# Value transposes in pairs between half tiles, and value scaling on ScalarE in a backward sweep

## The reference

```python
def mixer(xs_, ctx):                     # second block
    z, xx, bx, cx, dtx, u = ssm_project(hx, w_in, conv_w, conv_b, dt_bias)
    y_f = ssd_chunked(xx, dt_f, a_f, bx, cx, s_f)       # forward scan
    y_b = ssd_chunked(rev(xx), rev(dt_b), a_b, rev(bx), rev(cx), s_b)
    y = y_f + rev(y_b) + d_skip * xx
    y = rmsnorm(y * silu(z), groups of 512)             # two groups
    pm = pool_mixer(u, pool_w, pool_scale)              # box means minus u, then a matmul
    return concat([y, pm]) @ w_out

def ssd_chunked(xs, dt, a, b, c, h0):    # per chunk of 128 tokens, 16 heads of 64
    y_off = (c @ state) * exp(acs)                      # what earlier chunks give
    state = state * exp(acs[last]) + b.T @ (xs * weight)  # weight: one number per token and head
    y_diag = (c @ b.T * decay) @ (xs * dt)              # inside the chunk
```

## Time and profile before

| what | value |
|---|---|
| median of three runs | 2821.09 us |
| profiled execution | 2826.55 us, its span 2824.8 us |
| TensorE busy | 2659.1 us, 94% of the span |
| VectorE busy | 1638.1 us, 58% |
| GpSimd busy | 995.2 us, 35% |
| ScalarE busy | 609.5 us, 22% |
| backward sweep | about 1544 to 1717 us of the span |
| phase 6, up to the second product loop | about 1849 to 1980 us |

### The profile page before, as it was taken

One profiled execution on the slowest core, in us unless ns is written; L12 is line 12 of the kernel. 1 busy time (PEld: TensorE's weight loads), 2 busy tenths in 40 slices (PEclk: granted clock), 3 DMA queues, 4 the chain that ended last, 5 costly groups with the idle time before them and its releaser, 6 DMA issues. The chain is left out here.

```text
span 2824.8 us, 32083 instructions
## 1 busy us (share of the span) xinstructions
PE 2659.1 (94%) x12350; PEld 2143.5 (76%) x12350; DVE 1638.1 (58%) x2219; ACT 609.5 (22%) x884; POOL 995.2 (35%) x523
## 2 busy tenths in 40 slices
PE   8889999999999999987888999889989999999997
PEld 5778777778888888866776766678767888888885
DVE  6887555756556665676846995653375222222248
ACT  4222242311110011133232104532131110001111
POOL 2122125554333343541212331113645333333353
PEclk9999999999999999998999999989999999999998
DMA  4111142222322332231001332351332111111123
GB/s 138 40 52 44 52 142 82 97 82 97 97 90 89 104 97 94 94 103 64 31 30 38 104 112 75 79 197 45 112 97 83 52 52 45 52 45 52 45 75 105
DMA packets 87332, 224.68 MB, mean 80 GB/s; under 512 B 27392, under 2 KB 30592, under 8 KB 87232
## 3 DMA queue, kind: packets, MB, share of 16 engines
q1 hardware_dynamic: 51232, 168.61, 18.0%
q10 hardware_dynamic: 34848, 50.50, 5.7%
q0 software_dynamic: 1152, 4.19, 0.9%
HBM read 193.79 MB, written 28.31 MB: 79 GB/s over the span
## 5 line engine op out<-in xcount | busy, mean ns | idle before, releaser
L221 POOL CAST w_hi<-w_raw 128x1024 fp32r<-128x1024 f32 x254 | 289.4, 1139 | 1691.1 <-PE ps L234 1672.0
L230 PE MATMUL ps<-a_hi,w_hi 128*128 128x512 f32 x2080 | 698.5, 404 | 51.2 <-PEq L3028 14.6
L223 POOL TENSOR_TENSOR w_lo<-w_raw,w_hi 128x1024 fp32r<-128x1024 f32 x254 | 695.7, 2739 | 20.3
L232 PE MATMUL ps<-a_lo,w_hi 128*128 128x512 f32 x2080 | 680.2, 395 | 0.0
L234 PE MATMUL ps<-a_hi,w_lo 128*128 128x512 f32 x2080 | 679.1, 394 | 0.0
L230 PEld LDWEIGHTS ps<-a_hi,w_hi 128*128 128x128 f32 x2080 | 391.2, 192 | 157.7 <-issue 68.6
L234 PEld LDWEIGHTS ps<-a_hi,w_lo 128*128 128x128 f32 x2080 | 396.7, 191 | 85.2
L232 PEld LDWEIGHTS ps<-a_lo,w_hi 128*128 128x128 f32 x2080 | 397.5, 191 | 83.9
L232 PE MATMUL ps<-g_b,w_hi 128*128 128x512 f32 x1216 | 412.1, 390 | 0.0
L230 PE MATMUL ps<-g_b,w_hi 128*128 128x512 f32 x1088 | 363.8, 392 | 11.5 <-DVE g_b L1812 11.5
L234 PE MATMUL ps<-g_b,w_lo 128*128 128x512 f32 x1088 | 361.5, 389 | 0.0
(11 more groups left out here) (476 smaller groups left out, 2641.2 us busy)
## 6 DMA issues: line engine op xcount, KB each, us to landing
w_raw<-in_wstream SPq DMA_DIRECT2D x254, 512.0 KB, 3.5
ada_w<-in_ada_w ACTq DMA_DIRECT2D x25, 512.0 KB, 3.5
ada_w_b<-in_ada_w ACTq DMA_DIRECT2D x25, 512.0 KB, 3.4
x_res_b<-in_xT SPq DMA_DIRECT2D x2, 2048.0 KB, 11.4
x_block<-x_res_b SPq DMA_DIRECT2D x16, 256.0 KB, 3.1
y_by_token<-y ACTq DMA_DIRECT2D x8, 512.0 KB, 3.3
z_rows<-ada_w ACTq DMA_DIRECT2D x8, 512.0 KB, 2.6
u_rows<-pad ACTq DMA_DIRECT2D x8, 512.0 KB, 4.3
```

What stands on the lines that cost most here:

```text
L221: pool.tensor_copy(k.w_hi[:, s, :], k.w_raw[:, s, :]).then_inc(k.w_high, 1)
L223: pool.tensor_tensor(k.w_lo[:, s, :], k.w_raw[:, s, :], k.w_hi[:, s, :].bitcast(F32), ALU.subtract).then_inc(k.w_split, 1)
L230: pe.matmul(o, w_hi, a_hi[:, c], start=first, stop=False)
L232: pe.matmul(o, w_hi, a_lo[:, c], start=False, stop=False)
```

## The change

Phase 5: VectorE no longer multiplies the values by their own weight, and no longer weighs the next chunk's values in the sweep. ScalarE does both, head by head: 16 ACTIVATEs of 64 columns each, with a per-partition scale (`own_values`, `weigh_next`). A new semaphore `y_own` lets VectorE's sum wait for the first. Phase 6: the 64 value transposes no longer stand in one piece between the halves of pooled tile 0. They stand in four pairs of groups: behind tile 0, between the halves of tile 1, behind tile 1, between the halves of tile 2. The column sums of the squares move from behind tile 1 to behind tile 2, the spread from the middle of tile 2 to the middle of tile 3. ScalarE's squares and copies are put in the matching order.

```diff
+            def own_values(i):
+                if i:
+                    act.wait_ge(s["y_back"], 16 * i)
+                else:
+                    act.wait_ge(s["x_done"], CC)
+                for h in range(SSM_HEADS):
+                    ins = act.activation(heads(y_even[:, :])[:, h, :], values(NC - 1 - i)[:, h, :], ACT.Copy,
+                                         scale=v.own[:, NC - 1 - i, h:h + 1])
+                ins.then_inc(s["y_own"], 1)
+
+            def weigh_next(i):
+                c, r = (NC - 2 - i, 1) if i < NC - 2 else (0, 0)
+                act.wait_ge(s["x_done"], back + BWD_JOBS * i + 2)
+                for h in range(SSM_HEADS):
+                    ins = act.activation(heads(xw[:, :])[:, h, :], values(c)[:, h, :], ACT.Copy,
+                                         scale=v.w_st[:, c, SSM_HEADS * r + h:SSM_HEADS * r + h + 1])
+                ins.then_inc(s["xw_ready"], 1)
...
+            own_values(0)
             act.wait_ge(s["cleared"], 2)
             for i in range(NC):
                 c, t = NC - 1 - i, KT - 1 - i
                 act.wait_ge(s["y_ready"], i + 1)
                 act.dma_start(d.y_tok[c, :, :], y_even[:, :]).then_inc(s["y_back"], 16)
+                if c:
+                    weigh_next(i)
                 n = u_tile(i)
...
                 if t % 2 == 0 and t:
                     load_area(t // 2 - 1)
+                if i + 1 < NC:
+                    own_values(i + 1)
...
-                dve.wait_ge(s["y_back"], 16 * i)
-                ch.link(tt(heads(y_even[:, :]), values(c), bc(v.own[:, c, :], 2, HDIM), ALU.mult))
                 dve.wait_ge(s["x_done"], back + BWD_JOBS * i + 1)
                 tt(heads(back_tmp), heads(Xf[0]), per_head(v.e_acs, c, 1), ALU.mult).then_inc(x_free[0], 1)
                 dve.wait_ge(x_free[0], back // 2 + i + 1)
+                dve.wait_ge(s["y_own"], i + 1)
                 tt(y_even[:, :], y_even[:, :], back_tmp, ALU.add).then_inc(s["y_ready"], 1)
                 if c:
                     dve.wait_ge(s["x_done"], back + BWD_JOBS * i + 2)
                     sum_state(c, 1, 1)
-                    if c > 1:
-                        weigh(c - 1, 1)
-                    else:
-                        weigh(0, 0)
...
-        def value_transposes():
+        def value_transposes(first):
             pe.wait_ge(s["y_in"], 16)
-            for t in range(KT):
+            for t in range(first, first + 2):
...
             if m == 0:
-                value_transposes()
                 pe.wait_ge(s["plo"], KT)
-            if m == 2:
+            if 1 <= m <= 2:
+                value_transposes(4 * m - 2)
+            if m == PG - 1:
                 spread(0)
                 spread(1)
...
-            if m == 1:
+            if m < 2:
+                value_transposes(4 * m)
+            if m == 2:
                 square_sums(0)
                 square_sums(1)
...
+        squares(range(0, 2))
         pooled_part(0)
+        squares(range(2, 4))
         pooled_part(1)
+        squares(range(4, KT))
+        pooled_part(2)
         root(0)
         root(1)
         for t in range(0, 4):
             high(t)
-        pooled_part(2)
+        pooled_part(PG - 1)
```

More of the change, by code:

```diff
@@ L2390, in phase5 @@
         s = signals(nc, ctx, "p5", "chain xw_ready moving_ready d_done chosen e_ready w_ready cb_done cb_ready off_done fore_ready "
-                                   "st_done state_ready diag_done y_ready y_back y_out0 y_out1 u_in0 u_in1 u_in2 u_in3 z_out d_out "
+                                   "st_done state_ready diag_done y_ready y_own y_back y_out0 y_out1 u_in0 u_in1 u_in2 u_in3 z_out d_out "
                                    "dhi dlo x_done x_free0 x_free1 cleared area_in pooled")
@@ L2914, in scalar, with squares @@
         act.wait_ge(s["dlo"], len(LATE))
[L2915 to L2919, removed]
+        def squares(ts):
+            for t in ts:
+                act.wait_ge(x_free[t % 2], t // 2 + 1)
+                if t >= 2:
+                    act.wait_ge(s["added"], t - 1)
+                act.activation(w.tmp[:, t % 2, :], yz[:, t, :], ACT.Square).then_inc(s["sq"], 1)
         def pooled_part(m):
@@ L2942, in scalar @@
             high(t)
-        pooled_part(2)
+        pooled_part(PG - 1)
         for t in range(4, KT):
             high(t)
-        for m in range(3, KT):
+        for m in range(PG, KT):
             pooled_part(m)
```

## The result

The changed kernel takes 2831.64 us (2824.51 to 2836.71, seven runs), the kernel before, beside it, 2821.09 (2818.49 to 2828.03, seven runs). The ratio over all these runs is 1.0028, with an interval of 1.0016 to 1.0040: 7.9 us slower, between 4.5 and 11.3 (the two medians alone lie 10.6 apart). The interval lies above 1; the difference is just under the 0.3% taken as the bound of what can be told from no change. The profiled spans are 2824.8 and 2831.2 us, 6.4 apart.

A forecast was written before the change was run, and what follows sets the result against it. The prediction took TensorE to bound the kernel, with short stretches where another engine feeds it late. The sweep's +16 and phase 6's -10 gave +6 us on the median of 2821.09, so 2827 us, own range 2819 to 2834.

The forecast's parts named there:

- the +16: Phase 5, backward sweep: with both sets of scalings on ScalarE it ends 16 us later.
- the relief: Sweep: with VectorE partly idle, some stretching of its two-SBUF-input operations goes; -3 us, between 0 and -5.
- The pairs: Phase 6: value transposes in four pairs between half pooled tiles, none waiting; 10 us gained.
- The later spread: Phase 6: sums, roots and spread one pooled tile later in TensorE's order cost nothing, with 28 us of cover.
- the 12 that the forecast named for that case: Phase 6: upper end of the gain, 12 us, if the half clock around the sums goes too.
- The set of 3.95 us: Sweep: one set of 16 64-column ACTIVATEs on ScalarE takes 3.95 us.
- the rival of 4.8 us: Sweep: a set costs 4.8 us, the 128-column spacing; +18 net, 2839 us; chance 16%.
- The ring of 11.4 us a step: Sweep: chain pooled tile, own set, sum, weighing set, copy, pooled tile; 11.4 us a step beside the pooled tile.
- these three terms: Sweep: step 0 +1.7, steps 1 to 6 +22.7, step 7 -9.1; sum +15.3 us.
- the late TensorE of +3.5: Sweep: late state for steps 3, 5, 6 slows TensorE, so the last u tile is late; +3.5 us, 0 to +6.
- Nothing of the 16 us is taken back: Forward scan: it cannot start without the sweep's end, so it recovers none of the 16 us.
- The faster rival: Sweep: sets lie beside other work, TensorE alone bounds it; needs sets under about 2.8 us; 2804 us; chance 12%.

The follow-up runs named there:

- the sixth experiment: Kernel before, with all 64 value transposes in one piece moved from between the halves of pooled tile 0 to behind it; 2824.01 us, ratio 1.0006.
- the last experiment: Changed kernel with the own-weight set right behind the copy of the u tile and the weighing back on VectorE; 2813.61 us, ratio 0.9966 to the kernel before.
- the second experiment: Kernel before with only the scaling moved to ScalarE, phase 6 left as it was; 2840.2 us, ratio 1.0056.
- the fourth experiment: Changed kernel with the weighing set moved behind the copy of the u tile; 2829.15 us, ratio 1.0016 to the kernel before.
- The third experiment: Changed kernel with the own-weight set moved right behind the copy of the u tile; 2814.05 us, ratio 0.9958 to the kernel before.

## Why the prediction was right, point by point

**The direction and the size.** Forecast +6 on 2821.09; the spans differ by 6.4, the runs by 7.9. The two terms were +16 and -10, and they measured +17.2 and -10.1. Each came from the place and the cause that the forecast named. That the +16 came so close is in part luck: inside it one term was too small and another was not paid, as the point on the relief below shows.

**The pairs: right.** Not one pair waits. The first starts 16.5 us behind the third group of pool products (1895.57 - 1879.09, the latter TensorE's first row there); by the forecast's 1879.3 and the 1862.79 of before it was to be 16.5. The later spread was hidden, with 26.7 us of cover where 28 were worked out, and pooled tile 3 is copied out 10.1 us sooner from the phase's start. The forecast gave the 4.21 us wait and the region pace one sum and could not split them; the sixth experiment splits them. The lower clock behind the column sums stayed in the kernel after (24 products in 7.17 us, as before); in the last experiment it is gone and the stretch 11.7 us shorter, close to the 12 that the forecast named for that case.

**The set of 3.95 us: right.** It measured 3.92 to 3.94 (up to 3.97 in the experiments); the forecast had it from the slope between two shapes and the spacing of a third. The single 64-column form takes 333 ns (forecast 338). With that the rival of 4.8 us falls.

**The ring of 11.4 us a step: right in kind and size.** Steps 3 and 5 took 11.2 and 11.15 us from pooled tile to pooled tile. Steps 2, 4 and 6, which have an area load ahead of the own-weight set, took 13.5, 13.9 and 14.4 where 12.6 were expected, because their sums were stretched to 2.3, 2.75 and 3.3 us; step 1 took 14.1 where 11.4 + 3.4 were expected. Counted between the ends of pooled tiles (26.4, 148.8 and 172.3 us behind the sweep's first product before; 28.9, 175.0 and 189.5 after, for steps 0, 6 and 7), step 0 is longer by 2.6 us (forecast 1.7), steps 1 to 6 by 23.7 (forecast 22.7), and step 7 shorter by 9.1 (forecast 9.1). Together +17.2, where these three terms were to be +15.3. Of step 0, the forecast's own terms come to 1554.6 and not 1554.2, so to +2.0; and 0.9 of the 2.6 us belongs to the sweep's first products, which ran at a lower clock in this trace: in the second experiment, with the same sweep, step 0 is longer by 1.7.

**The relief of -3 us and the late TensorE of +3.5: one offset, the other hidden.** The relief came in the pooled tiles: those of steps 1 to 6 took 67.8 us in place of 70.8. But the forecast had the sum at 1.22 us in its ring, and it took 2070 ns in the mean, more than the 1549 of before: GpSimd's splitting falls on other operations, not on the idle time. The forecast's reading of the earlier trace rows, that every operation with two SBUF inputs is stretched, was too wide; the own-weight multiplication has two and took 1.22 us each time, since no subtraction of GpSimd lay beside it. With the relief counted, the forecast's ring gave +12.3 us where +17.2 were measured.

TensorE's waits for the state came as forecast (about 5, 8 and 2 us; measured 7.21, 7.21 and 2.50, and behind each of the long ones four products take 3.7 us), and the last u tile is done at 1726.34, inside the forecast's 1724 to 1727. What the forecast missed is when the ring asks for it, not at 1722 but at 1726.96, when ScalarE has issued y:

```profile
1725.72 0.61 PE L234 MATMUL ps<-a_hi,w_lo 128*128 128x512 f32 x2
```

```profile
1726.53 0.33 ACTq L2636 DMA_DIRECT2D y_by_token<-y  x1
1726.96 1.02 ACT L2642 ACTIVATE big<-ps 128x1024 f32<-128x1024 f32 x1 [1.79 <-DVE y L2773]
```

So the +3.5 was not paid. The ring and TensorE's lateness, which the ring causes, lie 0.6 us apart at the sweep's end. In the fourth experiment, whose ring is shorter, the last step does wait for TensorE; no run parts the two in the kernel after.

**"Nothing of the 16 us is taken back": not contradicted.** The forward scan took 2.1 us less than in the trace of before. At its end the kernel before ran a group of 32 products in 7.09 us that takes 4.96 after. But the sixth experiment, with the code of before up to there, shows the same two things, 144.1 us and 5.15. So the change is not the cause. In the traces of this study the scan took from 144.0 to 150.4 us, and why was not tested.

**The faster rival: its condition was wrong.** It asked for sets under 2.8 us and offered 2804 us, 17 under before. The third experiment is 11.9 under before (6.5 to 16.9) with sets of 3.96 us, so the place can decide as well as the length. The Trainium skill, Perfetto Trace Analysis, Optimizing Scalar/DVE Operations, says that offloading from a saturated VectorE to ScalarE may make sense. The traces agree only with the "may": one order of the same 240 instructions gave +17.2 us in the sweep, another -4.7.

**Left open.** Why the pairs alone gained 5.6 us in the total (at most 9.9) when their stretch gained 10.1. Untouched stretches of that trace differ by -3.2 and +2.6 us, which nearly cancel, and the scatter of the executions was not explained.

## What to carry to other kernels

Before work is moved to an engine that is nearly idle, write down what each instruction ahead of it in that engine's queue waits for, and who waits for the instruction behind it: if both are the engine that was to be relieved, the move builds a ring, and its length is the sum of both sides. Then move the work to a place in the queue where the other engine has something else to do, here behind the copy of the u tile, and ask who waits for the moved work itself: the own-weight set lost nothing by that place, the weighing set came late to TensorE. A burst paced by few buffers is better cut into pieces of that many buffers, with independent work between them that lasts longer than freeing them: here 5.5 us of products against 2.35 us of VectorE.

## What the runs showed of the hardware

A 128x1024 operation of VectorE with two SBUF inputs took from 1.22 to 3.4 us in the sweep, and each one over 1.3 us ran beside a subtraction of GpSimd; with an input in PSUM it took 1.22 us each time (line 2770 above, mean 1218 ns), also where it lay wholly beside the subtraction (line 2700 at 1576.41 in the trace before, 1.22 us). VectorE and GpSimd after, at one such place:

```profile
1663.93 2.75 DVE L2773 TENSOR_TENSOR y<-y,big 128x1024 f32<-128x1024 f32 x1 [4.79 <-ACT y L2618]
```

```profile
1663.26 2.34 POOL L223 TENSOR_TENSOR w_lo<-w_raw,w_hi 128x1024 fp32r<-128x1024 f32 x1
```

The sum lies beside GpSimd's subtraction and takes 2.75 us where the one at 1684.29, with GpSimd idle, took 1.23. The Trainium skill, SBUF — State Buffer, Who interferes with whom, gives a port pair shared by VectorE and GpSimd as the only place of contention, held by one at a time; these rows agree, and show the price, 1.5 us for one operation here.

Of TensorE: behind idle times of 7.21 us four products took 3.71 and 3.75 us (granted clock 0.50, the lower of the two clock levels), behind one of 2.50 us they took 1.95 (1.00). The length of the wait alone does not tell: behind the same 2.73 us at the start of the sweep they took 1.95 us in the trace before (1.00) and 2.92 in the trace after (0.61 over the first 3.9 us).
